# Keeping the results of two expert pairs, not one, in on-chip memory at the end of a mixture-of-experts block

## What is computed

```python
def hierarchical_moe(h, w_rg, b_rg, w_re, b_re, w_gate, w_up, w_down):
    ...                      # each token gets 1 of 4 groups, in it 2 of 8 experts: comb (T, 4, 8)
    y = jnp.zeros_like(h)
    for g in range(N_EXPERT_GROUPS):
        a = jnp.einsum('td,edf->tef', h, w_gate[g])
        b = jnp.einsum('td,edf->tef', h, w_up[g])
        act = jax.nn.silu(a) * b * comb[:, g, :, None]
        y = y + jnp.einsum('tef,efd->td', act, w_down[g])
    return y

    ...                      # end of second_block
    x = x + gt_f[:, None, :] * ffn.reshape(B, S, D)
    return rmsnorm(x, norm_final_g)
```

## Time and profile before

| | us |
|---|---|
| median of 3 executions (1873.5 to 1875.53) | 1873.64 |
| the profiled execution, its own time | 1875.62 |
| its span, first to last instruction | 1873.9 |
| PE busy (90% of the span) | 1684.0 |
| DVE busy (40%) | 751.7 |
| from the end of up(15) to the end of the span, by the timeline | about 27 |

### The profile page before, as it was taken

The page is one execution under the profiler, slowest core; times in us unless marked ns, Lnnn a source line. Parts: engine busy times, 40 slices in busy tenths (PEclk is TensorE's granted clock), DMA queues, the critical chain, the costliest instruction groups (busy, mean ns, idle before and its releaser), DMA issues. The chain is left out here.

```text
span 1873.9 us, 21968 instructions
## 1 busy us (share of the span) xinstructions
PE 1684.0 (90%) x8078; PEld 955.9 (51%) x8078; DVE 751.7 (40%) x1907; ACT 435.1 (23%) x1081; POOL 112.4 (6%) x130
## 2 busy tenths in 40 slices
PE   6999999899998999999987777778899999998777
PEld 2656555476667888756322222222368555633222
DVE  5445445765556654463111111010555554321114
ACT  3323223214452000023111010101222431222211
POOL 1100000100000000000000000000100000011100
PEclk9999999999999999999999999999999999899999
DMA  8742335951120622476999999999712234699996
GB/s 346 265 157 101 121 136 200 405 195 43 43 76 24 268 91 90 174 323 231 420 428 427 427 427 427 426 427 426 277 45 75 91 139 202 235 419 426 426 425 246
DMA packets 67879, 474.61 MB, mean 253 GB/s; under 512 B 11381, under 2 KB 12597, under 8 KB 45632
## 3 DMA queue, kind: packets, MB, share of 16 engines
q1 hardware_dynamic: 51168, 398.76, 52.7%
q0 software_dynamic: 15456, 70.32, 9.6%
q10 hardware_dynamic: 1152, 4.19, 0.5%
HBM read 458.58 MB, written 34.64 MB: 263 GB/s over the span
## 5 line engine op out<-in xcount | busy, mean ns | idle before, releaser
L2243 PE MATMUL moe_ps<-moe_up,moe_hg 128*64 128x512 f32 x1536 | 354.4, 608 | 96.2 <-DMA moe_up<-in_exp_up 36.7
L2243 PEld LDWEIGHTS moe_ps<-moe_up,moe_hg 128*64 128x64 f32 x1536 | 111.2, 139 | 333.8 <-issue 231.1
L2275 PE MATMUL moe_ps<-moe_down,moe_midT 128*64 128x512 f32 x720 | 163.8, 598 | 21.5 <-DMA moe_down<-in_exp_down 19.2
L534 PE MATMUL mx_pair<-hT,hg_w 128*128 128x512 f32 x336 | 149.1, 596 | 1.7 <-DMA hg_w<-in_w_hg 1.7
L2351 ACT ACTIVATE moe_sig<-moe_ps 128x512 f32<-128x512 f32 (+1 forms) x32 | 15.7, 491 | 521.6 <-PE moe_ps L2243 521.6
L2380 DVE COPY moe_midT<-moe_ps 128x512 f32<-128x512 f32 (+1 forms) x32 | 17.9, 558 | 258.8 <-PE moe_ps L2256 258.8
L2390 DVE SCALAR_TENSOR_TENSOR moe_res<-moe_ps,moe_route_slot_share,moe_gain 128x512 f32<-128x512 f32 x64 | 45.1, 746 | 178.5 <-PE moe_ps L2275 178.5
L2275 PEld LDWEIGHTS moe_ps<-moe_down,moe_midT 128*64 128x64 f32 x720 | 49.4, 136 | 115.0 <-issue 86.6
L534 PEld LDWEIGHTS mx_pair<-hT,hg_w 128*128 128x128 f32 x336 | 62.1, 190 | 74.2 <-issue 73.4
L2372 DVE TENSOR_TENSOR moe_mid<-moe_sig,moe_ps 128x512 f32<-128x512 f32 (+1 forms) x32 | 17.7, 554 | 136.8 <-PE moe_ps L2243 134.3
L557 PEld LDWEIGHTS mx_pair<-hg_w,hT 128*128 128x128 f32 x512 | 58.3, 192 | 4.1 <-issue 3.3
(11 more groups left out here) (476 smaller groups left out, 2628.1 us busy)
## 6 DMA issues: line engine op xcount, KB each, us to landing
moe_down<-in_exp_down SPq DMA_DIRECT2D x44, 2048.0 KB, 37.3
moe_up<-in_exp_up SPq DMA_DIRECT2D x31, 2048.0 KB, 37.8
moe_up<-in_exp_gate SPq DMA_DIRECT2D x31, 2048.0 KB, 37.9
moe_up<-in_exp_in SPq DMA_DIRECT2D x31, 2048.0 KB, 32.9
rest_w<-in_mod_rest POOLq DMA_DIRECT2D x16, 1536.0 KB, 9.6
hg_w<-in_w_hg SPq DMA_DIRECT2D x32, 512.0 KB, 3.8
rest_w<-in_mod_rest POOLq DMA_DIRECT2D x8, 2048.0 KB, 8.6
xn<-in_w_merge SPq DMA_DIRECT2D x32, 512.0 KB, 4.3
```

Source lines behind the costliest of these rows:

```text
L534: last = pe.matmul(proj[bank][:, :], w[s][:, kc, :], k.hT[:, kc, :], start=(kc == 0), stop=(kc == KC - 1))
L2243: last = pe.matmul(self.up_ps[u][e * SLOTS:(e + 1) * SLOTS, :], self.hg[m % 2][:, kc, e * SLOTS:(e + 1) * SLOTS], w[:, e, kc % 4, :], star ...
L2275: last = pe.matmul(self.res_ps[side][e * SLOTS:(e + 1) * SLOTS, :], self.midT[:, f, e * SLOTS:(e + 1) * SLOTS], w[:, e, side * 512:(side + ...
```

## The change

`kept_pairs` becomes 2 in the second experts' stage. Pair 14 is no longer scattered: POOL drains and raises `early_stored` once the scatters of pairs 0 to 13 have landed. `AddOut` makes two one-hot matrices, so `place` runs two comparisons on DVE. PE gets four more calls of `add`, one for each chunk (`pair_before`), with the rows of pair 14 in `res[0]`: for chunk 0 before turn_mid(15), for chunk 1 before down(15), for chunks 2 and 3 just before `rows(2)` and `rows(3)`. What SP reads back keeps its size.

```diff
-        self.kept_pairs = 1
+        self.kept_pairs = 2 if self.NU == 1 else 1
...
+            if isinstance(j, int) and self.NU == 1:
+                added.pair_before(pe, 0)
             turn_mid(j, PAIRS - 1)
+            if isinstance(j, int) and self.NU == 1:
+                added.pair_before(pe, 1)
             if isinstance(j, int) and self.NU == 2:
                 added.tokens(pe, 1, (1,))
             down(j, PAIRS - 1)
...
+    def pair_before(self, pe, c):
+
+        pe.wait_ge(self.experts.S["res_ready"], PAIRS - 1)
+        self.add(pe, c, self.onehot[0][:, c * P:(c + 1) * P], self.experts.res[0])
+
...
+        if not one_pass and self.store is not None:
+            self.pair_before(pe, 0)
+            self.pair_before(pe, 1)
         self.tokens(pe, 2)
         pe.wait_ge(last_ready, 1)
         for c in range(TC):
             if c == 3:
                 self.tokens(pe, c)
             if self.store is not None:
-                rows(c, 0, stop=True).then_inc(S["added"], 1)
+                if c >= 2:
+                    self.pair_before(pe, c)
+                rows(c, 1, stop=True).then_inc(S["added"], 1)
                 continue
```

## The result

The changed kernel takes 1878.97 us (median of 20 executions) against 1875.34 us of the kernel before on the same occasions: ratio 1.0022, interval 1.0016 to 1.0028, so **+4.1 us (3.0 to 5.3)**. The two medians themselves lie 3.6 us apart. The forecast was +4.9 us, slower by more than 0.2%; the interval, 0.16% to 0.28%, lies mostly above that border and not wholly.

What follows compares the result with a forecast made beforehand. The read path through DVE and PE both bound the end, 0.14 us apart. Calls of 1.56 and 3.43 us, less 0.14, plus 0.1, sum to 4.95, carried as +4.9 onto the median: 1878.5 us, range 1876.5 to 1880.5.

Steps and rivals of the forecast that it cites:

- What bounds the kernel: End of the program: the read path through DVE and the PE path are both the bound, 0.14 us apart.
- The removal: POOL's scatter of pair 14 goes; read starts 3.1 us earlier, last chunk lands 0 to 3.1 earlier; worth 0.14 us.
- Chunk 0: Added PE call before turn_mid(15): takes 1.91 us, the idle gap hides all but 0.32 us.
- Chunk 1: Added PE call between turn_mid(15) and down(15): takes 1.91 us, down(15) 1.56 us late, chunk 0's 0.32 included.
- Chunks 2 and 3: Added PE calls after last_ready, where PE has no gap: 2 x 1.72 = 3.43 us, nothing hidden.
- The lead of 0.14 and the two halves: At total(3): read path leads PE by 0.14 us; total(3)'s halves take 0.1 us more when started on a signal.
- What follows total(3) stays whole: After total(3): output(1) and output(2) stand behind it in DVE's order, so the 9.1 us to the span's end stay.
- DVE's slack: On DVE before total(3): total(2) ends 3.3 us before total(3) can start; that slack is lost.
- Cheaper calls: Rival, added PE calls: 0.90 us a call instead of 1.72, so +1.9 us, 1875.5; 3 in 100.
- a hidden call of chunk 1: Rival, before down(15): chunk 1's call costs nothing, so +3.4 us, 1877.0; 6 in 100.
- the read as bound: Rival, end of the program: end follows the read, 0 to 3.1 us earlier, 1870.5 to 1873.6; 4 in 100.
- The collision with the last weights: Rival, transfers: earlier read delays pair 15's down weights, adding 0.8 to 2.6 us, 1879.3 to 1881.1; 6 in 100.

Runs made afterwards that it cites:

- run without calls: Changed kernel without its four added product calls on PE, read still waiting for pair 13 only; ratio to before 1.0003 (0.9994 to 1.0012).
- tokens(1) in the gap: Kernel before with tokens(1) moved from between the halves of up(15) to before turn_mid(15); ratio to before 0.9994 (0.9984 to 1.0003).
- run with the outputs first: Changed kernel with output(1) and output(2) ahead of total(3) in DVE's order; end 33.01 us after up(15)'s second half against 35.7, one profiled execution.
- run with the late read: Changed kernel with pair 14 scattered too and the read waiting for it, as before; ratio to before 1.0024 (1.0015 to 1.0033).

## Why the prediction was right, point by point

- **What bounds the kernel.** Right, and it was the step that mattered: the chain of waits named the read, the waits of total(0) and total(1) named PE. Relieving the read alone (run without calls) gave nothing in the timed runs and 0.14 us at total(3) when the clock's fall is taken off. Relieving PE alone gave 0.12 us (tokens(1) in the gap) and 0.24 us (no identity product for chunk 3, the fall taken off). The loaded PE lost all that was loaded on it behind its last idle stretch.
- **The removal.** The read was issued 3.11 us earlier, as said. It landed 0.75 us earlier in its first chunk and 2.3 in its third. Its last transfer was issued at 1848.8 and took 11.7 us, before at 1847.2 and 12.5 us, so the last chunk, of which the forecast spoke, landed 2.4 us earlier, inside the 0 to 3.1 given and above the 1.5 taken. It was worth nothing either way.
- **Chunk 0:** 0.32 forecast, 0.23 measured. **Chunk 1:** 1.56 with chunk 0, 1.31 measured. Both were forecast too large, for two reasons: a call between other products costs 1.82 us from start to start here (1849.85 to 1851.67, 1851.88 to 1853.70), not the 1.91 of tokens(1) (tokens(2) in the earlier trace rows had 1.82 too), and the turning gives way after 0.21 instead of 0.28.
- **Chunks 2 and 3:** 3.43 forecast, 3.43 measured. The records stand 0.429 us apart in the sixteen from 1859.10 to 1865.97 too. That decides against the sustained figure of the Trainium skill (TensorE: Matmul & The Clock Gate, Back-to-back issue gap) for these fp32 records; twice its isolated figure fits.
- **The lead of 0.14 and the two halves:** total(3) 1.92 after rows(3), its successor 1.43 after its start instead of 1.34. As said. Sum to there 4.70 in place of 4.95.
- **What follows total(3) stays whole:** nearly. The stores took 0.24 us longer, so that the tail is 4.94 us longer. That it agrees with the 4.95 forecast is luck: two misses of a quarter us cancel. The run with the outputs first says that this part isn't a constant: how the stores are spread moves it by 1.5 us.
- **DVE's slack:** 3.3 forecast, 3.47 found, though `both(1)` ate 1.35 us that the forecast didn't know of. In the run with the late read, where it did not, total(0) and total(1) waited for PE again (0.84 and 0.43 us) and the slack was 3.54: the 1.35 us went into such waits.
- **The rivals.** Cheaper calls, a hidden call of chunk 1, the read as bound: each would have shown at total(3) and didn't. The collision with the last weights didn't come: down(15) never waited for `moe_last` in any of the fourteen profiles.
- **What the sum left out.** The timed difference, 4.1 us, lies below the tail's 4.9, though its interval takes 4.9 in. One candidate with the right sign and size is the fall of the clock: of six profiled executions that leave PE's idle time before turn_mid(15) open, two had it (1.64 and 1.60 us), of eight that fill it none. At two in six that is 0.5 us on the mean, and +4.4 us would be left. That is argued and not shown. If the falls had nothing to do with the idle stretch, both would still lie among those six executions with a chance of about one in six; neither of the two executions is one of the kernel before itself; and the timed runs don't carry the clock of this stretch.
- **The time itself.** 1878.5 us was forecast and 1878.97 measured. That this is within 0.5 us is partly luck: the kernel before took 1875.34 us over the 20 executions and not 1873.64 as in the first three, so a starting point 1.7 us too low made up for a difference that was 1.3 us too large (4.9 against 3.6 between the medians).

## What to carry to other kernels

Before starting a transfer earlier because a chain of waits ends on it, measure by how much it came last: the next engine in line may be 0.1 us behind, and work that is added behind its last idle stretch to free the transfer is paid in full. Price each added instruction by the start-to-start distance of its own kind in the trace, and find each idle stretch that it can fall into; the calls that fell into idle time cost 1.3 us for two, the ones behind the last wait 3.4. And when an engine gets slack that it can't use, its order should change with it: two lines of DVE's order were worth 2.7 us of tail in the changed kernel, in the one execution that was profiled with them.

## What the runs showed of the hardware that I had not expected

**PE's clock fell right behind a short idle stretch, in two executions of six.** 1.52 us idle, 0.44 us of turning and 0.51 us idle were followed in two of six executions by some 3.3 us at a granted clock of 0.50 (1.2 GHz), in which the sixteen records of down(15) took 5.2 us from start to start instead of 3.59. The same instructions in four other executions ran at 1.00 throughout. That the idle time is the cause is not shown. The single idle stretch of 1.46 us before down(14), which all fourteen executions have, was followed by a down product of 3.65 us, at full clock, every time.

**DVE and POOL excluded each other where both read two SBUF tensors.** Seen in every kernel in which two such operations overlapped by more than 0.3 us: `both(1)` 1.98 to 3.38 us instead of 1.23 when POOL had begun first, `output(0)` up to 3.48 instead of 1.28, POOL's addition 3.33 and 3.43 instead of 2.35 when DVE had. `total`, which reads one operand from PSUM, kept its 1.29 us beside POOL (total(1) at 1858.27 beside POOL's addition at 1857.28). A held operation of DVE ended 1.1 us after POOL's end, and POOL's held addition 2.2 us after DVE's, each close to its own length (1.23 to 1.28 and 2.35 us), as if it had done nothing until the other was through. The Trainium skill says the same (SBUF — State Buffer, section Who interferes with whom): a DVE instruction with two SBUF inputs contends with a GpSimd instruction that reads SBUF, because its second input comes through the read interface that the two share; the shared pair of ports is an exclusive lock, and the order of issue decides who is blocked. The runs show the exclusion and the order, by the times above; the ports they don't show. The forecast took POOL's addition for harmless, which was right for the end and wrong for the reason: it cost 1.35 us that happened to be covered.

**The last stores took longer when they bunched.** From the end of output(3) to the end of the span it was 3.4 us in the one execution in which the other chunks' stores had landed before, and 4.4 to 5.0 us in the thirteen others, with stores just in front.
